# Hybrid decoder layer on one core: group norm sums of three retention heads moved from four TensorE products to VectorE adds and one product, at later steps

## What is computed

```python
    o, S_new = _retention(qh, kh, vh, S0.astype(jnp.float32), n_lead)
    omu = jnp.mean(o, -1, keepdims=True)
    ovar = jnp.mean(jnp.square(o - omu), -1, keepdims=True)
    on = ((o - omu) * lax.rsqrt(ovar + EPS)).reshape(B, T, D_V) * ret_gn_g.astype(jnp.float32)
    y_b = (on * jax.nn.silu(g_ret.astype(jnp.float32))).astype(h.dtype) @ w_ret_out
```

## Time and profile before

| what | value |
|---|---|
| median of 3 runs | 805.98 us (805.79 to 806.58) |
| the profiled execution's own time | 805.64 us |
| its span | 803.7 us |
| TensorE matmul busy | 774.3 us, 96% |
| VectorE busy | 664.9 us, 83% |
| ScalarE busy | 508.4 us, 63% |
| granted TensorE clock, mean | 0.987 |
| norm products, L1756 and L1763 | 32 products as 64 records |

### The profile page before, as it was taken

One profiled execution on the slowest core, in us unless ns is written; L12 is line 12 of the kernel. 1 busy time (PEld: TensorE's weight loads), 2 busy tenths in 40 slices (PEclk: granted clock), 3 DMA queues, 4 the chain that ended last, 5 costly groups with the idle time before them and its releaser, 6 DMA issues.

```text
span 803.7 us, 12108 instructions
## 1 busy us (share of the span) xinstructions
PE 774.3 (96%) x4755; PEld 659.7 (82%) x4755; DVE 664.9 (83%) x891; ACT 508.4 (63%) x632; POOL 96.9 (12%) x120
## 2 busy tenths in 40 slices
PE   8989999999999999999699899999999999999994
PEld 5989999767676689999699894888888888888873
DVE  5698999767677879899867567988998899899987
ACT  7434446475767676345476363788888888888863
POOL 0100000233243200000002001011111211110000
PEclk9999999999999999999989999999999999999998
DMA  8945454689887836445348544799999999999972
GB/s 338 388 154 179 165 192 154 237 310 319 296 294 263 312 131 211 146 177 177 138 153 306 210 175 159 288 348 380 375 377 359 371 358 360 365 365 370 349 282 81
DMA packets 39173, 213.27 MB, mean 265 GB/s; under 512 B 7381, under 2 KB 7637, under 8 KB 19244
## 3 DMA queue, kind: packets, MB, share of 16 engines
q1 hardware_dynamic: 23268, 165.39, 55.3%
q0 software_dynamic: 15408, 45.71, 16.3%
q10 hardware_dynamic: 432, 1.31, 0.4%
HBM read 193.45 MB, written 31.65 MB: 280 GB/s over the span
## 4 chain that ended last, share of the span: by engine, by line
PE 86%; DVE 9%; ACT 3%; issue 1%; DMA 1%; DVEq 0%; ACTq 0%
PE bank L1580 35%; PE bank L1854 33%; PE bank L1692 3%; PE bank L1727 2%; DVE w_lo L1089 2%; PE bank L1638 2%; DVE conv L1136 2%; PE bank L1844 2%; PE bank L1742 1%; PE bank L1756 1%; PE bank L1763 1%; PE bank L1703 1%; ACT w_hi L755 1%; PE bank L1884 1%; PE bank L1606 1%
## 5 line engine op out<-in xcount | busy, mean ns | idle before, releaser
L1580 PE MATMUL bank<-h_hi,w_hi 128*128 128x264 f32 (+1 forms) x640 | 189.4, 296 | 3.4 <-DVE w_lo L1089 3.4
L1580 PE MATMUL bank<-h_lo,w_hi 128*128 128x264 f32 (+1 forms) x640 | 184.7, 289 | 0.0
L1580 PE MATMUL bank<-h_hi,w_lo 128*128 128x264 f32 (+1 forms) x640 | 184.6, 288 | 0.0
L1094 DVE TENSOR_TENSOR ring_lo<-raw,ring_hi 128x2048 fp32r<-128x2048 f32 x72 | 163.6, 2289 | 23.4 <-ACT ring_hi L762 23.4
L1089 DVE TENSOR_TENSOR w_lo<-raw,w_hi 128x1024 fp32r<-128x1024 f32 x112 | 136.8, 1221 | 38.7 <-ACT w_hi L755 38.4
L755 ACT ACTIVATE w_hi<-raw 128x1024 fp32r<-128x1024 f32 x112 | 117.9, 1052 | 69.7 <-PE bank L1580 69.4
L762 ACT ACTIVATE ring_hi<-raw 128x2048 fp32r<-128x2048 f32 x72 | 138.2, 1920 | 19.7 <-PE bank L1854 19.7
L1580 PEld LDWEIGHTS bank<-h_hi,w_hi 128*128 128x128 f32 x640 | 121.2, 189 | 8.8 <-DVE w_lo L1089 5.4
L1580 PEld LDWEIGHTS bank<-h_lo,w_hi 128*128 128x128 f32 x640 | 121.2, 189 | 0.6 <-issue 0.2
L1580 PEld LDWEIGHTS bank<-h_hi,w_lo 128*128 128x128 f32 x640 | 121.0, 189 | 0.0
L1136 DVE SCALAR_TENSOR_TENSOR conv<-u,vec,conv 128x256 f32<-128x256 f32 x240 | 101.6, 477 | 0.2
(11 more groups left out here) (283 smaller groups left out, 1492.7 us busy)
## 6 DMA issues: line engine op xcount, KB each, us to landing
raw<-weights SPq DMA_DIRECT2D x152, 1024.0 KB, 7.3
S_ring<-in_state_ret POOLq DMA_DIRECT2D x26, 512.0 KB, 6.6
out_ret_sample<-S_ring POOLq DMA_DIRECT2D x26, 512.0 KB, 6.5
S_five<-in_state_ret POOLq DMA_DIRECT2D x6, 512.0 KB, 4.9
out_ret_sample<-S_five POOLq DMA_DIRECT2D x6, 512.0 KB, 7.5
out_ret_prompt<-S_out POOLq DMA_DIRECT2D x8, 256.0 KB, 4.7
y_rows<-xg POOLq DMA_DIRECT2D x4, 512.0 KB, 5.7
raw<-y_rows SPq DMA_DIRECT2D x2, 1024.0 KB, 6.0
```

Of the source, the lines that this page charges most:

```text
L1094: dve.tensor_tensor(ring_view(ring_lo, k), raw[raw_slot(NCM + k)][:, :].rearrange("p (k n) -> p k n", k=4), ring_view(ring_hi, k).bitcast( ...
L1580: ins = pe.matmul(out, a[:, k, cols], b[:, k0 + k, :], start=first and k == 0 and j == 0, stop=last and k == ks - 1 and j == 2)
```

## The change

For heads 0 to 2 the four tiles are first added on DVE (two instructions: two tiles plus two tiles, then one plus one, into `gsq`), and TensorE takes one product of the sum. The adds for the mean stand at the old step of gm (k = 6, 10, 14), the product and the subtraction one step later (7, 11, 15); the adds for the variance at 8, 12, 16, and the product, root, reciprocal and scaling at 9, 13, 17, two steps later than before. Head 3 keeps its four products at 18 and 19. A new semaphore gsum_ready tells TensorE of the sums. The helper `halved` gets a destination and a count; the layer norm's calls do what they did.

```diff
+GM_AT, GV_AT, GM_SUM, GV_SUM = (7, 11, 15, 18), (9, 13, 17, 19), (6, 10, 14), (8, 12, 16)
...
-            if k >= 6 and (k - 6) % 4 == 0 and k <= 18:
-                add((("gm", (k - 6) // 4), "D"))
-            if k >= 7 and (k - 7) % 4 == 0 and k <= 19:
-                add((("gv", (k - 7) // 4), "A"))
+            if k in GM_AT:
+                add((("gm", GM_AT.index(k)), "D"))
+            if k in GV_AT:
+                add((("gv", GV_AT.index(k)), "A"))
...
-            def halved(src):
-
-                n = KT
+            def halved(dst, src, n):
+
                 while n > 1:
                     n //= 2
-                    ins = dve.tensor_tensor(ln_sq[:, 0:n, OUT], src[:, 0:n, OUT], src[:, n:2 * n, OUT], ALU.add)
-                    src = ln_sq
+                    ins = dve.tensor_tensor(dst[:, 0:n, OUT], src[:, 0:n, OUT], src[:, n:2 * n, OUT], ALU.add)
+                    src = dst
                     if n > 1:
                         link(ins)
-                ins.then_inc(csum_ready, 1)
+                return ins
...
+                    if k in GM_SUM:
+                        h = GM_SUM.index(k)
+                        evacuated(dve, ("ot", h))
+                        halved(gsq, oT[:, 4 * h:4 * h + 4, :], 4).then_inc(gsum_ready, 1)
+                    if k in GV_SUM:
+                        dve.wait_ge(osq_ready, GV_SUM.index(k) + 1)
+                        halved(gsq, gsq, 4).then_inc(gsum_ready, 1)
...
+                        if h < NH - 1:
+                            pe.wait_ge(gsum_ready, 2 * h + 1)
+                            b = opened(("gm", h))
+                            done(pe.matmul(b[:, OUT], cst("mean_v"), gsq[:, 0, OUT], start=True, stop=True))
+                        else:
+                            evacuated(pe, ("ot", h))
...
+                        if h < NH - 1:
+                            pe.wait_ge(gsum_ready, 2 * h + 2)
+                            b = opened(("gv", h))
+                            done(pe.matmul(b[:, OUT], cst("mean_v"), gsq[:, 0, OUT], start=True, stop=True))
```

More of the change, by code:

```diff
@@ L494, in build @@
         yy_in = [sem(f"yy_in{i}") for i in range(3)]
-        gf_in, csum_ready, csamp_done, ga_ready = sem("gf_in"), sem("csum_ready"), sem("csamp_done"), sem("ga_ready")
+        gf_in, gsum_ready, csum_ready, csamp_done, ga_ready = sem("gf_in"), sem("gsum_ready"), sem("csum_ready"), sem("csamp_done"), sem("ga_ready")
         zeroed, vw_ready, q_ready, yhi_last, ylo_last, fin_ready, sum_done = (sem(n) for n in (
@@ L920, in _ @@
                                             bank(("ot", h))[:, 0:32].rearrange("p (f n) -> p f n", f=4), ACT.Copy))
-                    if k >= 6 and (k - 6) % 4 == 0 and k <= 18:
-                        h = (k - 6) // 4
+                    if k in GM_AT:
+                        h = GM_AT.index(k)
                         evacuated(act, ("gm", h))
@@ L926, in _ @@
                         act.activation(gsq[:, :, OUT], oT[:, 4 * h:4 * h + 4, OUT], ACT.Square).then_inc(osq_ready, 1)
-                    if k >= 7 and (k - 7) % 4 == 0 and k <= 19:
-                        h = (k - 7) // 4
+                    if k in GV_AT:
+                        h = GV_AT.index(k)
                         seen(act, ("gv", h))
@@ L1303, in _ @@
                     dve.wait_ge(conv_step, KT * CW)
-                    halved(conv)
+                    halved(ln_sq, conv, KT).then_inc(csum_ready, 1)
                 if w == LN_MEAN:
@@ L1310, in _ @@
                     dve.wait_ge(csq_ready, 1)
-                    halved(ln_sq)
+                    halved(ln_sq, ln_sq, KT).then_inc(csum_ready, 1)
                 if w == LN_VAR:
@@ L1750, in _ @@
                         done(ins)
[L1751 to L1764, removed]
+                    if k in GM_AT:
+                        h = GM_AT.index(k)
+                        if h < NH - 1:
[4 more added lines that the diff above has]
+                            evacuated(pe, ("ot", h))
+                            b = opened(("gm", h))
+                            for et in range(4):
+                                ins = pe.matmul(b[:, OUT], cst("mean_v"), oT[:, 4 * h + et, OUT], start=et == 0, stop=et == 3)
+                            done(ins)
+                    if k in GV_AT:
+                        h = GV_AT.index(k)
+                        if h < NH - 1:
+                            pe.wait_ge(gsum_ready, 2 * h + 2)
+                            b = opened(("gv", h))
+                            done(pe.matmul(b[:, OUT], cst("mean_v"), gsq[:, 0, OUT], start=True, stop=True))
+                        else:
+                            pe.wait_ge(osq_ready, h + 1)
+                            b = opened(("gv", h))
+                            for et in range(4):
+                                ins = pe.matmul(b[:, OUT], cst("mean_v"), gsq[:, et, OUT], start=et == 0, stop=et == 3)
+                            done(ins)
                     if k in (20, 21):
```

## The result

| | before | changed |
|---|---|---|
| median of 16 runs each | 806.79 us (805.46 to 809.26) | 809.33 us (806.39 to 812.82) |
| ratio, 95% interval | | 1.0030 (1.0018 to 1.0041) |
| profiled execution, its span | 805.64, 803.7 us | 808.32, 806.5 us |
| mean granted clock | 0.987 | 0.982 |

The change costs 2.5 us where 1.3 were to be gained. It lies outside the range, 1.7 us above its upper end. Of the distance to the forecast of 804.7, 0.8 us is the kernel before itself, whose median is 806.79 here and was 805.98 in its first three runs. The stage itself looks much as forecast, up to its last stall; what stands behind that stall does not.

A forecast was written before the change was run, and what follows sets the result against it. TensorE was taken to bound the changed stage: 8.0 us saved, less stalls of 1.0, 2.25, 0.6 and 2.5 and four restarts, leaves 1.3 us; 804.3 for the profiled execution, forecast median 804.7 us, range 801.8 to 807.6.

The forecast's parts named there:

- What TensorE saves: Norm products of heads 0 to 2: six groups lose three products each at 0.445 us, 8.0 us in all.
- What DVE gets: Six pairs of adds on DVE at 1.17 us a pair, 7 us in all.
- First and second place: Steps 9 to 10 and 13 to 14: TensorE stalls 1.0 and 2.25 us for S(10) and S(14), ahead of samp_o.
- Third place: Steps 16 to 17: TensorE stalls 0.6 us for ACT's osb ahead of "ot" of head 3.
- Fourth place: Steps 17 to 19: TensorE stalls 2.5 us for the square ahead of head 3's variance products.
- four restarts of a waiting TensorE at some 0.1 us each: Allowance for TensorE resuming after the four stalls, taken off the gain along with the stalls to leave 1.3 us.
- A: Rival: DVE has room where the norm lands, so the whole 8.0 us saving stays; 798.0 us, chance 0.06.
- B: Rival: last stall only half and the one for osb none, gain 3.2 us; 802.8 us, chance 0.22.
- C: Rival: DMA-bound load of state 31 stays late, S(15) 3.2 us late, 1.9 us lost; 807.9 us, chance 0.12.
- D: Rival: another 1 to 3 us of delay in the same chains, such as single-product turns; 805.9 us, chance 0.15.
- E: Rival: root waits 1.4 us for a drain behind its table load at heads 1 and 2; 807.5 us, chance 0.

The follow-up runs named there:

- filled kernel: Changed kernel plus two idle products on TensorE ahead of its wait for head 3's square; 807.33 us, 0.9997 of the kernel before.
- move without sums: Changed kernel's later steps for heads 0 to 2, but four products each and no adds on DVE; 811.79 us, 1.0056 of the kernel before.
- head-2 kernel: Changed kernel with only head 2 summed on DVE at later steps, heads 0 and 1 as before; 810.57 us, 1.0049 of the kernel before.
- head 2, filled: Only head 2 summed at later steps, plus two idle products ahead of the wait for head 3's square; 810.53 us, 1.0035 of the kernel before.

## Why the prediction was wrong

**What TensorE saves: right.** The mean's single product shows 0.64 behind the broadcasts. That is not a dearer product: the group there took 1.98 for 1.78 as well, and 1.98 less 0.64 is 1.34, three products at 0.445. The lap from ot(5) to ot(9), in which TensorE waits for nothing, confirms it: seven products left it, 3.12 by the forecast's price, and it is 3.09 shorter. Only the single product behind "ot" is a tenth dearer: from "ot" of step 17 to the mean of head 3 it was 3.80 before and is 4.34.

**What DVE gets: right.** A pair of adds took 1.17 in the gap at 281.75, and 1.1 behind S(14), where it is on the path.

**First and second place: the chain right, the stall's end not.** I had S(10) end 11.4 us after step 9's broadcasts; it ended at 232.21 less 220.72, 11.5. I had S(14) end at 11.8; it was 268.72 less 256.70, 12.0. But `samp_o` ended 1.07 and 1.09 after them, where I counted 0.6 and 0.56. The rows say why (PE in order of time, the idle time before in brackets):

```profile
232.25 1.03 PE L1645 MATMUL bank<-S_ring,qm 128*8 128x512 f32 x4 [0.28 <-DVE S_ring L1274]
```

```profile
267.47 1.03 PE L1645 MATMUL bank<-S_ring,qm 128*8 128x512 f32 x4 [1.59 <-DVE S_ring L1274]
268.78 1.03 PE L1645 MATMUL bank<-S_five,qm 128*8 128x512 f32 x4 [0.28 <-DVE S_five L1274]
```

Eight records take 0.97 when they run through the earlier trace rows, four behind a wait take 1.03. **A restart costs 0.5 here, not the 0.1 of my estimate**, and the table of waits does not show it, since TensorE counts as busy. Each of the two late `samp_o` restarts twice. The first place cost 1.56 for 1.0 by the laps (-1.11, where six products less are -2.67).

**Third place: no stall, by a hair.** "ot" of head 3:

```profile
283.69 1.04 PE L1755 MATMUL bank<-con,osb 128*128 128x8 f32 x8
```

With T, the end of S(14), at 268.72 that is T + 15.0 (T + 15.1 by the end of the product ahead of it). I had TensorE at T + 14.6 and osb at T + 15.2. TensorE was half a microsecond later, by the restart, and osb was done at 283.62, T + 14.9, a little sooner than counted; so nothing was left to wait for.

**Fourth place: right to a tenth.** Square done at T + 26.7 by the forecast; the products start at 295.48, T + 26.76. TensorE arrives at T + 24.2 by the forecast; 295.48 less 2.60 is T + 24.16. The stall is 2.6 for 2.5.

**The sum up to here** is a gain of 0.75 by the laps (-3.09, -1.11, +0.31, +3.14) where I had 1.3: 0.55 short. The first two places cost 0.56 and 0.7 more than their stalls as counted, almost all of it restarts, and the last 0.2 more; against that stand the 0.4 set aside for restarts and the third stall, 0.6, which did not come.

**The step that failed** is "four restarts of a waiting TensorE at some 0.1 us each, my estimate", as the price of everything that follows a stall. Behind the last one the lap was 1.83 longer. About 0.25 is the restart at full clock: the variance products take 2.05 instead of 1.78 behind the short waits of the filled kernel and of the move without sums, and behind the head-2 kernel's wait of 2.6. The other 1.6 is the clock at the 1.2 GHz level; the forecast had no term for it. The earlier trace rows showed 1.00 in all thirteen windows, and I read it as a property of the stage; it was a property of a TensorE that never waited there. The same trace shows the other case 100 us later, at the layer norm: a wait of 4.55 us, and the clock at 0.50 around it (PE busy, then PEld, DVE, ACT, POOL, the granted clock, DMA share, GB/s):

```profile
401.79 1.25 PE L1779 MATMUL bank<-ln_sq,con 128*128 128x264 f32 x2 [4.55 <-DVE ln_sq L1108]
```

```profile
400.00:404.00 4.00, 2.21 (x8) 2.01 (x9) 3.21 (x5) 2.01 (x3) 0.00 (x0) 0.50 0.13 16
```

Gain 0.75, less 1.83, is the +1.08 of the stage. The median is +2.5. Over all executions the changed kernel is 1.1 shorter at full clock and loses 3.4 to the clock; 1.6 of the 3.4 is the stretch behind the last stall, and where the other 1.8 lie, and what brings them, is open.

The Trainium skill, TensorE: Matmul & The Clock Gate, HAM oscillation, tells of a loop whose waits for DMA between bursts of matmuls bring the clock down, so that each next burst starts cold. The trace agrees for a single wait (0.50 behind the 2.6 us), in four of the five profiles that have one of 2.6 or 2.9 us. A rival built on it with 1.6 to 1.9 us would have stood at about 806.5. I had none.

**The rivals.** A (saving whole) fell: the stalls are there. B (smaller stalls) fell but for the third. C (state load late) did not come: ACT scaled state 31 at 269.91 after 1.00 us of waiting, 5 us sooner than in the earlier trace rows. C's 807.9 is the nearest of the rivals to 809.33, but its mechanism did not act in the changed kernel. D was right that the same chains hold more delay, 0.55 us of it net, but from the restarts and not from its "turns of 0.65 per single product". E (drain behind the table load) is refuted again; load and root of head 2 on ACT:

```profile
285.85 1.28 ACT L933 ACT_TABLE_LOAD   x1
287.14 0.48 ACT L933 ACTIVATE rstd<-bank,con 128x264 f32<-128x264 f32 x1
```

## What to carry to other kernels

Price a new wait of TensorE in three parts: the wait, the restart of what follows (0.5 us for `samp_o`, 0.25 for the variance products), and, as behind the waits of 2.6 and 2.9 us here in four of five profiles, a stretch at half clock. Two small moves that were right in the ledger (8 us of products for 6.3 us of stalls) can lose by the last two parts. Look in the trace of before for the longest wait of TensorE, wherever it is, and read the clock behind it. Take the part of a saving that makes no wait: the three variance sums at the old steps gain 3.1 us, while all six sums at later steps lose 2.5; and where a wait can't be avoided, idle products ahead of it (not behind it) are worth a try: in the changed kernel they took the loss away, in the head-2 kernel they gained nothing.

## What the runs showed of the hardware

- Behind waits of 2.6 and 2.9 us ahead of head 3's variance products the granted clock fell to the 1.2 GHz level in four of five profiles, at a cost of about 1.6 us each besides the restart; in the fifth it stayed at 1.00. Behind waits of 1.59 us ahead of `samp_o` and of 2.0 us ahead of "ot" (head 2, filled) the windows read 1.00.
- Four matmul records of `samp_o`, 128x512, behind a wait of 0.28 us took 1.03 us, eight in a running stream 0.97.
- Two idle products took 1.88 us ahead of the wait at clock 1.00, and 3.54 behind it at 0.53.
